# Values of the gated recurrence computed feature by feature and transposed on TensorE, with the output fetches, the query fetch and the copies moved in their queues

## The chip, the cores and the metric

The kernel is one program on one core of a Trainium2 chip. The metric is the time of one execution on the device, in microseconds (us), as the median of several runs. The engines are named as the profile names them: PE is TensorE (PEld its weight loads), DVE is VectorE, ACT is ScalarE, POOL is GpSimd, and SP is the queue engine that issues most DMAs. [...]

## The reference

Two transformer-like blocks run one after the other on 512 tokens of width 1024. The change is in the second block, whose sequence has 16 meta tokens in front (528 tokens, `T2`). After a norm the tokens `z` are projected and fed into two mixers:

```
z = rmsnorm(h, mix_norm_g)
p = z @ w_in                                  # u | q | f | i | og | ga | gb, 1024 columns each
y_a = s5_mixer(p[u], ...)                     # state space model
y_b = hgrn2_mixer(p[q], p[f], p[i], p[og], lb, norm_g)
merged = sigmoid(p[ga]) * (y_a @ w_ssm_proj) + sigmoid(p[gb]) * (y_b @ w_hgrn_proj)

# hgrn2_mixer, per head of 128 features, chunks of 16 tokens
f = lb + (1 - lb) * sigmoid(f_logit);  cum = cumsum(log f) within a chunk
q_in = q * exp(cum);  k_in = (1 - f) * exp(-cum);  v = i_in
scores = where(causal, q_in @ k_in.T, 0);  o = scores @ v + q_in @ state
state = decay * state + k_out.T @ v
```

The part `i` (`i_in`, the values `v`) is needed with tokens on the partitions (`Vt`); `q` and `f` are needed with features on the partitions.

## The kernel before, in words

**Products in parts.** Each f32 weight tile of 128 x 1024 (a unit, 512 KB) is fetched by SP into one of two `stage` buffers, copied by ACT into `whi` (`split_hi`, L912), and DVE makes the rest `wlo = stage - whi` (`split_lo`, L2153); there are four pairs `whi`/`wlo`. A job of PE is three products (`whi*zhi`, `whi*zlo`, `wlo*zhi`) for each of 8 k tiles, into two PSUM banks (one for each half of the tokens), picked by the job's parity. `marks` counts finished jobs; `emptied[parity]` says that the job's PSUM has been read out. `ahead(name, j)`, called by ACT and by DVE before they serve job `j`, splits the unit that takes the buffers of the job before (four units further on). SP loads a unit when the one two before it has been split. All engines run their own program strictly in order, so the order in which the calls stand is the order of the work.

**Order around the change.** Jobs `u`, `q`, `f` (8 each), then the values `i0`, `i1`, then 8 `ga` jobs with the state space outputs between them, then `i2`, `i3`, then 8 heads with two gate jobs each (`og`, `gb`), then `glu`. `i0` to `i3` are each 256 features: five jobs (one for each of five token tiles of 128, the last overlapping), in which the token tile is the stationary operand and 256 weight columns stream (L1998, 24 matmuls a job). ACT copies each job's 128 x 256 from PSUM straight into `Vt` (`value_job`, L1266).

**State space side.** DVE runs a scan of 64 steps (L2752, L2757, L2759) up to the middle of `i1`, and between its steps `skip(b)` finishes the kernel tile of block `b` (`k_done`). The Toeplitz tile `TT` of a block is made by 8 shifting DMAs: 4 from SP (`shifted`, L842), 4 from ACT (`k_shift`, L1283), both after `k_done`. `outputs(b)` on PE (L1975, L1982) needs them; ACT copies its result to `Y5` (L1315), SP stores it (`y_store`), and when all 8 are stored SP fetches them back turned, as 64 small DMAs (`y_rows`, L854), which ACT's gelu needs later.

**Gates.** POOL waits for the last `outputs`, issues the fetch of `f` into `KH` and of `q` into `QH` (4 DMAs each, L3109), zeroes `sT` and `kout` (L3112, L3113) and signals `rmask_done`, for which DVE waits before anything of `i2` and PE before the heads. ACT makes the logs of 8 heads (`gate_log`, L1325) in the first four jobs of `i2`; DVE then a scan for each head (L2813, L2815); ACT the two exponentials (`gate_exps`, L1332, L1334) one head in each job of `i3`, where head `h` waits for `dec_done` of head `h-2`; DVE `into_gates` (L2800 to L2806), `decays`, and in the heads `own_scores` and the other masks (`sT_done`). PE's head `h`: `head_scores` (L2028), a gate job, `head_keys` (four transposes, L2038), `head_second` (L2048), `head_third` (L2058), a gate job, `head_values` of the head before (L2090, L2096; not in head 0), `head_deltas` (L2073). ACT copies the transposed keys (`ko`, L1373) and spills the gate jobs (L1258).

Of the kernel before, what the change touches and what calls it, by code (L numbers as in the profile page):

```python
# [13 lines left out]
P = 128  # L14
# [19 lines left out]
HEADS = 8  # L34
# [170 lines left out]
SPILLED = ["q", "f", "ga", "og", "gb"]  # L205
# [3 lines left out]
def emit(nc, A, out):  # L209
# [4 lines left out]
    with ctx:  # L214
# [121 lines left out]
        kout4 = at("kout4", [P, T1], 4 * CONST["mla"])  # L336
        rmask = at("rmask", [P, T2], 4 * CONST["mla"])
# [108 lines left out]
        lb_in, lb_sig, lb_done = sem("lb_in"), sem("lb_sig"), sem("lb_done")  # L446
# [300 lines left out]
        def _(sp):  # L747
# [62 lines left out]
            def weights(name, j):  # L810

                c0 = {"u": 0, "q": 1024, "f": 2048, "og": 4096, "ga": 5120, "gb": 6144}
                if name[0] == "i":
                    c = 3072 + 256 * int(name[1])
                    return [(lambda s: s[:].rearrange("p (k c) -> p k c", k=4), w_in2[:, 4 * j:4 * j + 4, c:c + 256])]
# [87 lines left out]
        def _(act):  # L903
# [314 lines left out]
            def ssm_angles():  # L1218
                act.wait_ge(s5_vec, 2)
                act.activation(v5[:, 3, :], v5[:, 3, :], ACT.Exp).then_inc(s5_exp, 1)  # L1220
                act.wait_ge(s5_vec, 3)
                act.activation(v5[:, 7:9, :], v5[:, 7:9, :], ACT.Sin).then_inc(s5_sin, 1)
                act.wait_ge(lb_in, 1)
                act.activation(gsc[:, 2, :], gsc[:, 2, :], ACT.Sigmoid).then_inc(lb_sig, 1)
# [37 lines left out]
            def value_job(c, j):  # L1262

                n = J["i%d" % c] + j
                act.wait_ge(marks, plan.full[n])
                act.activation(Vt[:, j, c * 256:(c + 1) * 256], ps[:, 2 * (n % 2), 0:256], ACT.Copy)\  # L1266
                   .then_inc(emptied[n % 2], 1)
# [37 lines left out]
            for c in range(2):  # L1305
                for j in range(TB2):
                    ahead("i%d" % c, j)
                    if (c, j) == (0, 0):
                        k_evac(1)
                    elif (c, j) == (0, 3):  # L1310
                        k_shift(1)
                    value_job(c, j)
# [23 lines left out]
            act.wait_ge(lb_done, 1)  # L1336
            for j in range(TB2):
                ahead("i2", j)
                if j < 4:
                    gate_log(2 * j)  # L1340
                    gate_log(2 * j + 1)
                value_job(2, j)
            for j in range(TB2):
                ahead("i3", j)
                gate_exps(j)
                value_job(3, j)
            for h in range(TB2, HEADS):
                gate_exps(h)
# [19 lines left out]
            for h in range(HEADS):  # L1368
# [10 lines left out]
                if h == 1:  # L1379
                    act.wait_ge(yT_in, 16 * KD * KD)  # L1380
                if 1 <= h <= 4:
                    for k in (2 * h - 2, 2 * h - 1):
                        act.activation(y5[:, k, :], y5[:, k, :], ACT.Gelu_apprx_tanh).then_inc(gelu_done, 1)
# [70 lines left out]
        def _(pe):  # L1454
# [3 lines left out]
            def products(n, T, ks, w, x_hi, x_lo, fresh=None):  # L1458

                last = None  # L1460
                for b, t0, t1 in halves(T):
                    out = ps[:, 2 * (n % 2) + b, 0:t1 - t0]
# [8 lines left out]
            def gemm(name, j, x_hi, x_lo, T, ks=KD, i=None, fresh=None):  # L1471
# [7 lines left out]
                products(n, T, ks, lambda a, k: a[u % NHL][:, k * P:(k + 1) * P], x_hi, x_lo, fresh)\  # L1479
# [506 lines left out]
            def value_jobs(c):  # L1986

                name = "i%d" % c
                for j in range(TB2):
                    n = J[name] + j  # L1990
                    wait_emptied(pe, n)
                    out = ps[:, 2 * (n % 2), 0:256]
                    for k in range(KD):
                        uu, o = (U[name] + k // 4) % NHL, (k % 4) * 256
                        if j == 0 and k % 4 == 0:
                            pe.wait_ge(split_done, U[name] + k // 4 + 1)
                        for a, x in ((whi, zhi), (wlo, zhi), (whi, zlo)):
                            mm = pe.matmul(out, x[:, k, TS2[j]:TS2[j] + P], a[uu][:, o:o + 256],  # L1998
                                           start=(k == 0 and a is whi and x is zhi), stop=(k == KD - 1 and x is zlo))
                    mm.then_inc(marks, 1)  # L2000
# [6 lines left out]
            value_jobs(0)  # L2007
            value_jobs(1)
            for b in range(NB5):
                outputs(b)  # L2010
                gemm("ga", b, zx(zhi), zx(zlo), T3)
                if b + 2 < NB5:
                    kernels(b + 2)
            value_jobs(2)
            value_jobs(3)

# [45 lines left out]
            def head_deltas(h):  # L2062
# [4 lines left out]
                else:  # L2067
                    wait_job_out(pe, J["i3"] + TB2 - 2)
                    wait_job_out(pe, J["i3"] + TB2 - 1)
# [36 lines left out]
            for h in range(HEADS):  # L2106
                head_scores(h)
                gate_job(2 * h)
# [38 lines left out]
        def _(dve):  # L2147
# [467 lines left out]
            def ssm_params(step):  # L2615
# [3 lines left out]
                if step == 0:  # L2619
# [7 lines left out]
                                      ALU.subtract).then_inc(lb_in, 1)  # L2627
# [30 lines left out]
                elif step == 4:  # L2658
                    product_re(BB[:, 0, :, :], *bb)
                    dve.wait_ge(lb_sig, 1)  # L2660
                    link(dve.tensor_scalar(gsc[:, 3, :], gsc[:, 2, :], -1.0, 1.0, ALU.mult, ALU.add))
                    dve.tensor_scalar(gsc[:, 0, :], gsc[:, 3, :], -1.0, None, ALU.mult).then_inc(lb_done, 1)
# [121 lines left out]
            for c in range(2):  # L2784
                for j in range(TB2):
                    ahead("i%d" % c, j)
                    scan(52 + 2 * (TB2 * c + j), 54 + 2 * (TB2 * c + j))
                    if (c, j) == (0, 2):
                        skip(1)
# [18 lines left out]
            dve.wait_ge(rmask_done, 1)  # L2808
            for j in range(TB2):
                ahead("i2", j)  # L2810
            for h in range(HEADS):
# [5 lines left out]
            for j in range(TB2):  # L2817
                ahead("i3", j)
# [24 lines left out]
            for h in range(HEADS):  # L2843
                into_gates(h)
                if h == 0:
                    decays(0, 1)
# [137 lines left out]
        def _(pool):  # L2984
# [120 lines left out]
            for name, tiles, done in (("f", KH, hgate_in), ("q", QH, qgate_in)):  # L3105
                for k in range(4):
# [93 lines left out]
```

## Time and profile before

| what | value |
|---|---|
| median of 3 runs | 1754.97 us (1750.53 to 1756.06) |
| the profiled execution's own time | 1754.68 us |
| its span | 1752.9 us |
| PE busy | 1696.5 us, 97% of the span |
| DVE, ACT, POOL busy | 1092.1, 745.3, 297.7 us (62%, 43%, 17%) |
| share of PE in the chain that ended last | 83% |

The profile page gives shares over the whole span. The views of the trace place things: the timeline lists the instructions of an engine in order of time, and a value in brackets behind one is how long the engine was idle before it and what released it. All times in the trace count from the start of the span.

### The profile page before, as it was taken

Reading aid. Unit: us, or ns where it says so; the run is one execution under the profiler, and the core shown is the slowest. Engines: PE = TensorE matmul, PEld = TensorE weight load, DVE = VectorE, ACT = ScalarE, POOL = GpSimd, SP = SyncE. Lnnn points to the kernel's source line nnn. Section 1 sums busy time; section 2 is a strip of 40 time slices with the busy share of each in tenths; the row PEclk is TensorE's granted clock in tenths of the full one; section 3 lists DMA queues with packets and bytes.
Section 4 is the critical chain, followed back from the end, with each engine's and each line's share of the span. In section 5 each row is a group of like instructions: output and inputs, shape, how many; then the busy total and the mean of one; then the engine's idle time right before and its main releaser. Section 6 shows DMA issues by size and latency. Waiting matters only on the chain.

```text
span 1752.9 us, 32409 instructions
## 1 busy us (share of the span) xinstructions
PE 1696.5 (97%) x12781; PEld 1506.5 (86%) x12781; DVE 1092.1 (62%) x1748; ACT 745.3 (43%) x1111; POOL 297.7 (17%) x286
## 2 busy tenths in 40 slices
PE   5999999999999999999999999999999999999998
PEld 4776756788888888799999999999999999989986
DVE  6756476677664577865868664343753766654633
ACT  4367575365332342632323545447233643322323
POOL 2112197310000001532005221210102000000002
PEclk8999999999999999999999999999999999999999
DMA  9363542433333332264435752332543233332332
GB/s 313 101 151 97 157 120 73 144 88 102 99 96 98 94 96 75 70 180 126 129 105 145 232 145 83 96 122 75 170 116 97 71 87 95 92 100 85 96 94 75
DMA packets 321167, 201.18 MB, mean 115 GB/s; under 512 B 51279, under 2 KB 303814, under 8 KB 320918
## 3 DMA queue, kind: packets, MB, share of 16 engines
q1 hardware_dynamic: 300976, 160.79, 32.3%
q0 software_dynamic: 7952, 24.83, 4.7%
q10 hardware_dynamic: 12118, 13.88, 2.3%
q8 instruction: 85, 1.39, 0.3%
q14 instruction: 36, 0.29, 0.1%
HBM read 177.75 MB, written 17.24 MB: 111 GB/s over the span
## 4 chain that ended last, share of the span: by engine, by line
PE 83%; DVE 6%; ACT 4%; SPq 2%; issue 2%; DMA 1%; POOL 1%; ACTq 0%; DVEq 0%; POOLq 0%
PE ps L1467 69%; SPq L854 2%; DVE wlo L2153 1%; PE ps L1608 1%; PE ps L1768 1%; PE ps L1794 1%; PE ps L1778 1%; PE ps L1667 1%; PE ps L1998 1%; PE ps L1682 1%; PE ps L1584 1%; ACT whi L912 1%; DMA xrow<-in_x_dram 1%; PE ps L1924 0%; PE ps L1536 0%
## 5 line engine op out<-in xcount | busy, mean ns | idle before, releaser
L1467 PE MATMUL ps<-zhi,whi 128*128 128x258 f32 (+2 forms) x2072 | 639.3, 309 | 2.8 <-DVE wlo L2153 1.4
L1467 PE MATMUL ps<-zlo,whi 128*128 128x258 f32 (+2 forms) x2072 | 634.0, 306 | 0.0
L1467 PE MATMUL ps<-zhi,wlo 128*128 128x258 f32 (+2 forms) x2072 | 632.7, 305 | 0.0
L1467 PEld LDWEIGHTS ps<-zhi,whi 128*128 128x128 f32 x2072 | 391.2, 189 | 27.7 <-DVE wlo L2153 2.9
L2153 DVE TENSOR_TENSOR wlo<-stage,whi 128x1024 fp32r<-128x1024 f32 x256 | 322.7, 1262 | 139.0 <-ACT whi L912 127.0
L1467 PEld LDWEIGHTS ps<-zlo,whi 128*128 128x128 f32 x2072 | 390.5, 188 | 19.5 <-issue 1.0
L1467 PEld LDWEIGHTS ps<-zhi,wlo 128*128 128x128 f32 x2072 | 391.1, 189 | 18.2
L912 ACT ACTIVATE whi<-stage 128x1024 fp32r<-128x1024 f32 x256 | 269.4, 1055 | 314.8 <-PE ps L1467 260.3
L1467 PE MATMUL ps<-ghi,whi 128*128 128x512 f32 x340 | 134.7, 396 | 0.0
L1467 PE MATMUL ps<-glo,whi 128*128 128x512 f32 x340 | 134.2, 395 | 0.0
L1467 PE MATMUL ps<-ghi,wlo 128*128 128x512 f32 x340 | 134.0, 394 | 0.0
L1201 ACT ACTIVATE ub<-ps 128x512 f32<-128x512 f32 (+1 forms) x88 | 52.6, 597 | 162.7 <-PE ps L1467 161.4
L3036 POOL TENSOR_TENSOR zu<-zu,sq 128x528 f32<-128x528 f32 (+1 forms) x18 | 31.6, 1758 | 425.5 <-ACT sq L920 424.6
L2566 DVE TENSOR_SCALAR cv<-ub,par 128x512 f32<-128x512 f32 (+1 forms) x88 | 49.0, 556 | 70.2 <-ACT ub L1201 70.2
L1211 ACT ACTIVATE ghi<-cv 128x512 f32 (+1 forms) x44 | 27.9, 634 | 124.4 <-DVE cv L2581 124.4
L1467 PEld LDWEIGHTS ps<-ghi,wlo 128*128 128x128 f32 x340 | 64.0, 188 | 15.0
L1467 PEld LDWEIGHTS ps<-ghi,whi 128*128 128x128 f32 x340 | 63.9, 188 | 14.7
L1467 PEld LDWEIGHTS ps<-glo,whi 128*128 128x128 f32 x340 | 63.9, 188 | 14.6
L2575 DVE SCALAR_TENSOR_TENSOR cv<-ub,par,cv 128x512 f32<-128x512 f32 (+1 forms) x88 | 66.3, 754 | 13.1 <-DVE cv L2569 6.7
L3029 POOL TENSOR_SCALAR pb<-pb,small 128x128 f32<-128x128 f32 (+3 forms) x64 | 72.8, 1156 | 9.5 <-DVE small L2456 9.2
L2482 DVE TENSOR_TENSOR xT<-ps,xT 128x512 f32 (+2 forms) x30 | 20.8, 692 | 85.1 <-PE ps L1467 85.1
L1258 ACT ACTIVATE spill<-ps 128x516 f32<-128x516 f32 (+1 forms) x40 | 24.1, 604 | 103.4 <-PE ps L1467 103.3
(426 smaller groups left out, 2836.2 us busy)
## 6 DMA issues: line engine op xcount, KB each, us to landing
stage<-in_w_up_dram SPq DMA_DIRECT2D x88, 512.0 KB, 3.8
stage<-in_w_in_dram SPq DMA_DIRECT2D x74, 512.0 KB, 4.0
stage<-in_w_down_dram SPq DMA_DIRECT2D x32, 512.0 KB, 4.0
ring<-in_w_ada_dram POOLq DMA_DIRECT2D x24, 512.0 KB, 4.4
adab<-in_w_ada_dram SPq DMA_DIRECT2D x16, 512.0 KB, 8.3
stage<-in_w_down_dram SPq DMA_DIRECT2D x16, 384.0 KB, 3.4
stage<-in_w_o_dram SPq DMA_DIRECT2D x8, 512.0 KB, 3.9
ring<-in_w_ada_dram SPq DMA_DIRECT2D x8, 512.0 KB, 3.8
```

What stands on the lines that cost most here:

```text
L854: sp.dma_start(y5[SH * g:SH * g + SH, k, :].rearrange("p (j c) -> p j c", j=LC), y_view[g])\
L912: act.activation(whi[u % NHL][:], stage[slot][:], ACT.Copy).then_inc(hi_done, 1)
L1201: act.activation(wide(ub[:, j % 2, 2:2 + T], T), acc(job, T), ACT.Copy).then_inc(emptied[job % 2], 1)
L1211: act.activation(ghi[c % 2][:, bass.ds(i * 2 + q, 1), 0:T].rearrange("p a t -> p (a t)"), cv[:, q, 1, 0:T], ACT.Copy).then_inc(ghi_done, 1)
L1258: act.activation(wide(spill[m % 2][:, T2 - T:T2], T), acc(n, T), fn).then_inc(emptied[n % 2], 1)
L1467: last = pe.matmul(out, w(a, k), x(k, t0, t1), start=(k == 0 and a is whi and x is x_hi), stop=(k == ks - 1 and a is wlo))
L2153: dve.tensor_tensor(wlo[u % NHL][:], stage[plan.w_load[u] % NST][:], whi[u % NHL][:].bitcast(F32), ALU.subtract).then_inc(split_done, 1)
L2482: ins = dve.tensor_tensor(x, acc(job, T), x, ALU.add)
L2566: link(dve.tensor_scalar(o, ub[:, g, 2:2 + T], tap(2), par[:, bass.ds(i * 2 + (ROW[f["cb"]] + ft), 1)], ALU.mult, ALU.add))
L2575: dve.scalar_tensor_tensor(out=o, in0=ub[:, g, 0:T], scalar=tap(0), in1=o, op0=ALU.mult, op1=ALU.add).then_inc(conv_done, 1)
L3029: pool.tensor_scalar(pb[:, t % 4, r, 0:w], pb[:, t % 4, r, 0:w], total(t, r, 32), None, ALU.mult)\
L3036: pool.tensor_tensor(square(n, 0), square(n, 0), square(n, 1 + j % 2), ALU.add).then_inc(acc_done, 1)
```

## The change

The values are now two groups of four ordinary jobs, `ia` and `ib` (128 features each, features on the partitions). ACT copies a job's result from PSUM to one of four column buffers `vcol` (`value_out`). PE transposes it with five f32 transposes back into the PSUM of the same job (`value_turn`), in the middle of the next job, between its two halves (`between`); the turns of values 3 and 7 stand behind `outputs(0)` and `head_scores(0)`. ACT then copies the turned tiles to `Vt` with two copies (`value_rows`) and frees the PSUM, and this copy stands ahead of the split of the next unit. The logs and exponentials are dealt out over the four jobs of `ib` (four heads, four heads, two, two). POOL fetches `q` only after job `ib` 0. `y_rows` are fetched in four pairs, each behind one unit of `og`. SP issues `shifted(1)` ahead of the loads of `ga` 0 and 1. The gelu of the state space outputs begins one head later.

```diff
-    p.shared("i0", 2, TB2)
-    p.shared("i1", 2, TB2)
+    p.gemm("ia", 4)
     p.gemm("ga", 8)
-    p.shared("i2", 2, TB2)
-    p.shared("i3", 2, TB2)
+    p.gemm("ib", 4)
...
+GATE_LOGS = [(0, 1, 2, 3), (4, 5, 6, 7), (), ()]
+GATE_EXPS = [(), (), (0, 1), (2, 3)]
...
+        vcol = [at("vcol0", [P, T2], ZUO + 2 * row), at("vcol1", [P, T2], RSO)] + spill
...
+        def value_no(m):
+            return (J["ia"] + m) if m < 4 else (J["ib"] + m - 4)
+        def value_cols(m):
+            return vcol[m % 2 + 2 * (m // 4)]
...
# SP
-            loads("i0", 0, 2)
+            loads("ia", 0, 2)
             shifted(0)
-            loads("i1", 0, 2)
+            loads("ia", 2, 4)
+            shifted(1)
             loads("ga", 0, 2)
-            shifted(1)
             loads("ga", 2, 4)
...
-                name, j = (("ga", b + 4) if b < 4 else ("i2", b - 4) if b < 6 else ("i3", b - 6))
+                name, j = ("ga", b + 4) if b < 4 else ("ib", b - 4)
                 loads(name, j, j + 1)
             y_store(NB5 - 1)
             loads("og", 0, 2)
             sp.wait_ge(ys_out, 16 * KD)
-            for k in range(6):
-                y_rows(k)
-            loads("og", 2, 3)
-            y_rows(6)
-            loads("og", 3, 4)
-            y_rows(7)
-            loads("og", 4, 8)
+            for k in range(4):
+                loads("og", k + 2, k + 3)
+                y_rows(2 * k)
+                y_rows(2 * k + 1)
+            loads("og", 6, 8)
...
# ACT
+            def value_out(m):
+                n = value_no(m)
+                act.wait_ge(marks, plan.full[n])
+                if m % 4 >= 2:
+                    act.wait_ge(vt_mm, m - 1)
+                if m in (4, 5):
+                    wait_spilled(act, "ga", m + 2)
+                act.activation(wide(value_cols(m)[:, :], T2), acc(n, T2), ACT.Copy).then_inc(vcol_done, 1)
+            def value_rows(m):
+                s = 2 * (value_no(m) % 2)
+                act.wait_ge(vt_mm, m + 1)
+                act.activation(Vt[:, 0:4, m * P:(m + 1) * P], ps[:, s, :].rearrange("p (b d) -> p b d", b=4), ACT.Copy)
+                act.activation(Vt[:, 4, m * P:(m + 1) * P], ps[:, s + 1, 0:P], ACT.Copy)\
+                   .then_inc(emptied[value_no(m) % 2], 1)
...
+            for m in range(4):
+                if m:
+                    value_rows(m - 1)
+                ahead("ia", m)
+                if m == 0:
+                    k_evac(1)
+                elif m == 1:
+                    k_shift(1)
+                value_out(m)
             for b in range(NB5):
...
                 ahead("ga", b)
+                if b == 0:
+                    value_rows(3)
...
+            for m in range(4, 8):
+                if m > 4:
+                    value_rows(m - 1)
+                ahead("ib", m - 4)
+                for h in GATE_LOGS[m - 4]:
+                    gate_log(h)
+                for h in GATE_EXPS[m - 4]:
+                    gate_exps(h)
+                value_out(m)
+            gate_exps(4)
+            value_rows(7)
+            for h in range(5, HEADS):
                 gate_exps(h)
...
# PE
+            def value_turn(m):
+                pe.wait_ge(vcol_done, m + 1)
+                n = value_no(m)
+                for b, t0 in enumerate(TS2):
+                    mm = pe.transpose(ps[:, 2 * (n % 2) + b // 4, (b % 4) * P:(b % 4) * P + P], value_cols(m)[:, t0:t0 + P],
+                                      const("ident"))
+                mm.then_inc(vt_mm, 1)
+            def value_job(m):
+                gemm("ia" if m < 4 else "ib", m % 4, zx(zhi), zx(zlo), T2,
+                     between=(lambda: value_turn(m - 1)) if m % 4 else None)
...
             for h in range(HEADS):
                 head_scores(h)
+                if h == 0:
+                    value_turn(7)
                 gate_job(2 * h)
...
# DVE
+            for m in range(4):
+                ahead("ia", m)
+                if m == 0:
+                    scan(52, 55)
+                    skip(1)
+                    scan(55, 57)
+                else:
+                    scan(52 + 5 * m, 57 + 5 * m)
...
+            dve.wait_ge(rmask_done, 1)
+            for m in range(4):
+                ahead("ib", m)
+                if m < 2:
+                    for h in range(4 * m, 4 * m + 4):
+                        gate_scan(h)
+                elif m == 2:
+                    into_gates(0)
+                    decays(0, 1)
+                    into_gates(1)
+            for h in range(2, HEADS):
                 into_gates(h)
-                if h == 0:
-                    decays(0, 1)
                 if h == 6:
                     own_scores(0)
...
# POOL
             for name, tiles, done in (("f", KH, hgate_in), ("q", QH, qgate_in)):
+                if name == "q":
+                    pool.wait_ge(marks, plan.full[J["ib"]])
                 for k in range(4):
...
+            pool.wait_ge(vt_mm, 4)
             pool.memset(kout[:, 0:T1], 0.0).then_inc(rmask_done, 1)
```

## Rows read from the trace of the kernel before

**Rows 1.** The profile page, first part: busy time of each engine.

```profile
PE 1696.5 (97%) x12781; PEld 1506.5 (86%) x12781; DVE 1092.1 (62%) x1748; ACT 745.3 (43%) x1111; POOL 297.7 (17%) x286
```

**Rows 2.** Timeline of PE: start, duration, line, count, idle before and its releaser.

```profile
889.39 0.39 PE L1998 MATMUL ps<-whi,zhi 128*128 128x256 f32 x1
...
904.94 0.39 PE L1998 MATMUL ps<-whi,zhi 128*128 128x256 f32 x1 [1.08 <-ACT Vt L1266]
...
919.34 1.16 PE L1975 MATMUL ps<-U,TT 128*64 128x66 f32 x32
...
937.96 1.16 PE L1975 MATMUL ps<-U,TT 128*64 128x66 f32 x32 [1.15 <-DMA TT<-K]
...
1017.32 1.19 PE L2028 MATMUL ps<-QH,KH 128*128 128x128 f32 x10
```

**Rows 3.** Waits of PE from 800 to 1200 us: total, times, longest.

```profile
PE ps L2073 <- ACT ko L1373: 1.4, 1, 1.4
...
PE ps L2028 <- DVE sT L2886: 0.6, 1, 0.6
```

**Rows 4.** The chain that ended last, from 800 to 1200 us.

```profile
1034.96 1.26 PE ps L2028 x10
```

**Rows 5.** Timeline of PE in head 1, gate jobs left out.

```profile
1041.89 0.60 PE L2038 MATMUL ps<-cst,kout 128*128 128x128 f32 x4
1042.42 0.69 PE L2048 MATMUL ps<-QH,KH 128*64 128x64 f32 x16
```

**Rows 6.** Timeline of ACT in jobs f and i0.

```profile
858.86 0.61 ACT L1258 ACTIVATE spill<-ps 128x528 f32<-128x528 f32 x1 [3.73 <-PE ps L1467]
...
864.71 0.61 ACT L1258 ACTIVATE spill<-ps 128x528 f32<-128x528 f32 x1 [3.72 <-PE ps L1467]
...
901.40 3.06 ACTq L1283 DMA_DIRECT2D TT<-K  x4
```

**Rows 7.** Timeline of SP: start, time until the last issue ended.

```profile
901.34 2.51 SPq L842 DMA_DIRECT2D TT<-K  x4
...
993.69 27.99 SPq L854 DMA_DIRECT2D y<-y_scratch  x48
```

**Rows 8.** The tile stage from 860 to 990 us: issue to landing of a unit.

```profile
DMA to landing us min/median/max: 3.5/4.9/14.9
```

**Rows 9.** Timeline of DVE in i0.

```profile
894.12 0.31 DVE L2752 TENSOR_TENSOR sc<-AA,S 128x128 f32<-128x128 f32 x1
...
899.84 0.27 DVE L2734 TENSOR_TENSOR dtmp<-cst,Dg 16x128 f32<-16x128 f32 x1
```

**Rows 10.** Timeline of POOL at the start of i2.

```profile
987.42 2.89 POOL L3109 DMA_DIRECT2D QH<-q_scratch  x4
...
991.45 0.55 POOL L3113 MEMSET kout<- 128x512 f32 x1
```

**Rows 11.** Timeline of DVE in i2, i3 and head 0.

```profile
992.02 1.23 DVE L2153 TENSOR_TENSOR wlo<-stage,whi 128x1024 fp32r<-128x1024 f32 x1 [5.97 <-POOL kout L3113]
...
1009.79 0.70 DVE L2800 TENSOR_TENSOR QH<-QH,ex 128x528 f32<-128x528 f32 x1
...
1027.40 1.22 DVE L2153 TENSOR_TENSOR wlo<-stage,whi 128x1024 fp32r<-128x1024 f32 x1
```

**Rows 12.** Timeline of ACT in i2 and i3.

```profile
989.13 0.60 ACT L1258 ACTIVATE spill<-ps 128x516 f32<-128x516 f32 x1 [4.34 <-PE ps L1467]
...
1015.06 0.65 ACT L1334 ACTIVATE LF<-LF 128x528 f32<-128x528 f32 x1
```

**Rows 13.** Windows of 2 us: length, busy and count of PE, PEld, DVE, ACT, POOL; granted clock; DMA.

```profile
730.00:732.00 2.00, 0.96 (x4) 0.61 (x5) 2.00 (x6) 1.54 (x5) 0.00 (x0) 1.00 0.01 4
...
1360.00:1362.00 2.00, 1.13 (x8) 0.83 (x7) 2.00 (x6) 1.98 (x4) 0.00 (x0) 0.98 0.00 0
1362.00:1364.00 2.00, 2.00 (x12) 2.00 (x11) 1.62 (x5) 1.97 (x6) 0.00 (x0) 0.50 0.00 0
1364.00:1366.00 2.00, 2.00 (x13) 2.00 (x13) 1.24 (x5) 1.99 (x4) 0.00 (x0) 0.67 0.00 0
```

More of the change, by code:

```diff
@@ L445, in emit @@
                                                          sem("ylo_done"), sem("ya_done"))
-        lb_in, lb_sig, lb_done = sem("lb_in"), sem("lb_sig"), sem("lb_done")
+        lb_step = sem("lb_step")
+        vcol_done, vt_mm = sem("vcol_done"), sem("vt_mm")
         lf_done, cum_done, ep_done, em_done, kin_done, dec_done = (
@@ L810, in weights @@
             def weights(name, j):
[L812 to L815, printed above, removed]
+                c0 = {"u": 0, "q": 1024, "f": 2048, "ia": 3072, "ib": 3584, "og": 4096, "ga": 5120, "gb": 6144}
                 if name in c0:
@@ L1222, in ssm_angles @@
                 act.activation(v5[:, 7:9, :], v5[:, 7:9, :], ACT.Sin).then_inc(s5_sin, 1)
-                act.wait_ge(lb_in, 1)
-                act.activation(gsc[:, 2, :], gsc[:, 2, :], ACT.Sigmoid).then_inc(lb_sig, 1)
+                act.wait_ge(lb_step, 1)
+                act.activation(gsc[:, 2, :], gsc[:, 2, :], ACT.Sigmoid).then_inc(lb_step, 1)
             def into_columns(b):
@@ L1304, in _ @@
                     k_shift(0)
[L1305 to L1312, printed above, removed]
+            for m in range(4):
[7 more added lines that the diff above has]
+                value_out(m)
             for b in range(NB5):
@@ L1334, in gate_exps @@
                 act.activation(LF[:, h, :], LF[:, h, :], ACT.Exp, scale=-1.0).then_inc(em_done, 1)
[L1336 to L1347, printed above, removed]
+            act.wait_ge(lb_step, 3)
+            for m in range(4, 8):
[10 more added lines that the diff above has]
+            for h in range(5, HEADS):
                 gate_exps(h)
@@ L1378, in _ @@
                     heads_out(h - 1)
-                if h == 1:
+                if h == 2:
                     act.wait_ge(yT_in, 16 * KD * KD)
-                if 1 <= h <= 4:
-                    for k in (2 * h - 2, 2 * h - 1):
+                if 2 <= h <= 5:
+                    for k in (2 * h - 4, 2 * h - 3):
                         act.activation(y5[:, k, :], y5[:, k, :], ACT.Gelu_apprx_tanh).then_inc(gelu_done, 1)
@@ L1456, in job, with products @@
                 pass
-            def products(n, T, ks, w, x_hi, x_lo, fresh=None):
+            def products(n, T, ks, w, x_hi, x_lo, fresh=None, between=None):
                 last = None
                 for b, t0, t1 in halves(T):
+                    if b and between:
+                        between()
                     out = ps[:, 2 * (n % 2) + b, 0:t1 - t0]
@@ L1469, in products, with gemm @@
                 return last
-            def gemm(name, j, x_hi, x_lo, T, ks=KD, i=None, fresh=None):
+            def gemm(name, j, x_hi, x_lo, T, ks=KD, i=None, fresh=None, between=None):
                 n, u = J[name] + j, U[name] + j
@@ L1478, in gemm @@
                     wait_emptied(pe, n, i)
-                products(n, T, ks, lambda a, k: a[u % NHL][:, k * P:(k + 1) * P], x_hi, x_lo, fresh)\
+                products(n, T, ks, lambda a, k: a[u % NHL][:, k * P:(k + 1) * P], x_hi, x_lo, fresh, between)\
                     .then_inc(marks, 1)
@@ L1984, in outputs @@
                 mm.then_inc(y_mm, 1)
[L1986 to L2000, printed above, removed]
+            def value_turn(m):
[8 more added lines that the diff above has]
+                     between=(lambda: value_turn(m - 1)) if m % 4 else None)
             for j in range(8):
@@ L2006, in _ @@
             kernels(1)
-            value_jobs(0)
-            value_jobs(1)
+            for m in range(4):
+                value_job(m)
             for b in range(NB5):
                 outputs(b)
+                if b == 0:
+                    value_turn(3)
                 gemm("ga", b, zx(zhi), zx(zlo), T3)
@@ L2013, in _ @@
                     kernels(b + 2)
-            value_jobs(2)
-            value_jobs(3)
+            for m in range(4, 8):
+                value_job(m)
             def head_scores(h):
@@ L2067, in head_deltas @@
                 else:
-                    wait_job_out(pe, J["i3"] + TB2 - 2)
-                    wait_job_out(pe, J["i3"] + TB2 - 1)
+                    wait_job_out(pe, value_no(6))
+                    wait_job_out(pe, value_no(7))
                 for b in range(4):
@@ L2626, in ssm_params @@
                     dve.tensor_tensor(gsc[:, 2, :], par[:, ROW["lb"]:ROW["lb"] + 8], par[:, ROW["lb"] + 8:ROW["lb"] + 16],
-                                      ALU.subtract).then_inc(lb_in, 1)
+                                      ALU.subtract).then_inc(lb_step, 1)
                 elif step == 1:
@@ L2783, in _ @@
                     skip(0)
[L2784 to L2789, printed above, removed]
+            for m in range(4):
[6 more added lines that the diff above has]
+                    scan(52 + 5 * m, 57 + 5 * m)
             for b in range(NB5):
@@ L2806, in into_gates, with gate_scan @@
                 dve.tensor_tensor(KH[:, h, :], KH[:, h, :], LF[:, h, :], ALU.mult).then_inc(kin_done, 1)
[L2808 to L2811, printed above, removed]
+            def gate_scan(h):
                 dve.wait_ge(lf_done, h + 1)
@@ L2816, in _ @@
                    .then_inc(cum_done, 1)
-            for j in range(TB2):
-                ahead("i3", j)
             def decays(h0, h1):
@@ L2841, in own_scores @@
                                     ps[:, 4, :].rearrange("p (b t) -> p b t", b=4)).then_inc(sT_done, 1)
-            for h in range(HEADS):
+            dve.wait_ge(rmask_done, 1)
+            for m in range(4):
+                ahead("ib", m)
[7 more added lines that the diff above has]
+            for h in range(2, HEADS):
                 into_gates(h)
-                if h == 0:
-                    decays(0, 1)
                 if h == 6:
```

8 lines of the change are left out of this document (2 added, 6 removed).

## Prediction, made before the changed kernel was run

> **What bounds the kernel now.** I read the page first: PE is busy 97% of the span [rows 1], so the end moves only with PE's own work and its gaps. The view of waits, cut to the stretch of the change, then shows how small its gaps are: about 5 us in 400, among them 2.0 us in head 0 [rows 3]. The timeline of PE gives the two stretches that the change rebuilds. The values `i0`, `i1` take from 889.39 to `outputs(0)` at 919.34, 29.95 us with a wait of 1.08 us in it; `i2`, `i3` take from the end of `ga` 7 at 989.1 to the first `head_scores` at 1017.3, 28.2 us without a gap [rows 2, 12]. Last I read the queues of ACT, SP, DVE and POOL in the same stretches, because each engine works in its written order, and a PE with short gaps can be held by any of them.
>
> **PE's work.** An ordinary job of 48 products takes 5.86 us (from spill to spill, 858.86 to 864.71) [rows 6]. Four transposes of the same form as the new ones take 0.53 us from their start to that of the next group [rows 5], so five take 0.66 us; if each took its full 0.27 us one behind the other it would be 1.35 us, which is the upper end. The group of four values with its three inner turns is 4 x 5.86 + 3 x 0.66 = 25.4 us, against 28.9 us (29.95 less the wait) and 28.2 us before. With the two outer turns of 0.66 us the work of PE falls by 3.5 + 2.8 - 1.3 = 5.0 us. That is the gain if nothing is late.
>
> The Trainium skill (TensorE: Matmul & The Clock Gate, Part 4: PE-mode transpose) gives about 275 ns for one 128 x 128 transpose inside a kernel. Taken as a spacing it would make 40 of them 11.0 us instead of 5.3 us; the rows agree with it as the length of one, but their starts lie closer.
>
> **The group ia: ACT is held by a load.** `shifted(1)` now stands ahead of the load of `ga` 0 in SP's queue, and it waits for `k_done`. Before, DVE ended six steps of the scan between 894.12 and 899.84 (0.95 us each), and the shifts went out at 901.34 [rows 9, 7]. Now three steps stand ahead, so they go out at 898.5 and SP is free 2.5 us later, at 901.0. Only then is the load of `ga` 0 issued; a unit lands 3.5 to 4.9 us after its issue [rows 8], I take 4.5 us: 905.5. ACT's queue for `ia` 1 is: `value_rows(0)` (done about 899.7), the split of `ga` 0, `k_shift(1)`, `value_out(1)`. The split waits for the landing and ends at 906.6; the four issues of `k_shift` take 3.06 us [rows 6], to 909.8; the copy of 0.6 us ends at 910.4. PE wants turn 1 at 889.39 + 2 x 5.86 + 0.66 + 2.93 = 904.7. It stands still for 5.8 us (4.8 to 6.2 over the range of landings), in the middle of job `ia` 2. What was behind cover before: the split of `ga` 0 came only at `i1`, long after its landing. DVE is queued behind the same split; it ends its last scan step at about 916, before `outputs(0)`. The group then takes 25.4 + 5.8 = 31.2 us instead of 29.95: 1.25 us lost.
>
> In the `ga` stage the 1.15 us that PE waits at 937.96 for shifted tiles [rows 2] shrink, since DVE has one split (1.2 us) less ahead of `skip(2)`; but turn 3 (0.66 us) and the output of `kernels` after it push the same chain. From `outputs(0)` to `outputs(2)` I count 0.36 us won. The rest of that stage keeps its order.
>
> **The group ib: DVE is held by POOL.** Let T be the start of `ib` 0 (989.1 in the old trace, by the end of `ga` 7 [rows 12]). POOL's queue is `f` fetch, `q` fetch, memsets, `rmask_done`. From the first issue of `q` at 987.42 to the last memset's end at 992.0 are 4.6 us [rows 10]. The `q` fetch now waits for the end of `ib` 0, T + 5.9, so `rmask_done` comes at T + 10.5 instead of T + 2.9. DVE has its wait for it in front of everything of `ib`: the split, eight scans, two more splits, the gates. From there to the first `into_gates` were 17.8 us (992.02 to 1009.79) [rows 11], with the same eight scans and three splits as now: T + 28.3. From that to the end of ACT's exponentials of head 3 were 5.9 us (1009.79 to 1015.71) [rows 11, 12]: T + 34.2. In the old order nothing of PE hung on them. Now `value_out(7)` stands behind the exponentials of heads 2 and 3, turn 7 behind `value_out(7)`, and the first gate job behind turn 7. The copy ends at T + 34.8, the turn at T + 35.5. PE's own work would bring it there at T + 25.4 + 1.2 + 0.66 = T + 27.3. A smaller wait lies inside: `value_out(6)` stands behind a split, a table load and four exponentials, and turn 6 waits some 0.6 us for it; it is covered by the larger one.
>
> Before, the first gate job started at T + 29.4. It is 6.1 us late. Of this 2.0 us come back, the two waits of head 0 [rows 3]: they came from 48 `y_rows` issues in one piece (28 us, 0.58 us each [rows 7]) ahead of `og` 2 and 3, and 16 of them between units cost 9.3 us, less than two gate jobs. With 5.9 us for head 0 less those waits, `head_scores(1)` stands at T + 50.0 instead of T + 45.9 (1034.96 [rows 4]): 4.1 us lost. DVE's gates and decays ended at 1027.40, T + 38.3 [rows 11]; 7.6 us later and with one more split between them they end at T + 47, and the split of `og` 3 and two masks (2.2 us) make it ready for `head_scores(1)` at T + 49, so it is not far from being the bound itself. Later heads have no wait that I find: each `og` unit lands before its split is wanted.
>
> **The clock.** Both stalls end in a long gap of PE: 5.8 us in `ia`, and in `ib` 3.7 us idle, 1.2 us of `head_scores`, 3.7 us idle. In the old trace the granted clock was 0.50 and 0.67 (the 1.2 GHz level) in the two windows from 1362, after PE had been busy 1.13 of 2 us from 1360; that is 1.7 us of work lost. But from 730 to 732 PE was busy 0.96 of 2 us and the clock stayed at 1.00 [rows 13]. I take one such loss for each stall, 2 x 1.7 = 3.4 us, with 0 and 3.4 us as ends.
>
> The Trainium skill (TensorE: Matmul & The Clock Gate, Why this matters for your kernels) warns that a long gap between bursts of matmuls puts the array back at half rate. By it both stalls cost the loss above, as in the sum; without it the sum would be 3.4 us smaller. The trace of before holds a case of each kind.
>
> **The rest at nothing.** The column copies and `value_rows` (0.6 and 0.8 us) are ACT's, which has gaps of over 3 us in each job; without them they would cost PE a wait at each turn. The gelu one head later has four heads of slack. The number of units and bytes is the same.
>
> **The sum.** 1.25 - 0.36 + 4.1 = 5.0 us, and 3.4 us for the clock: 8.4 us. The profiled execution took 1754.7 us (span 1752.9 and 1.8 around it), close to the median of 1755.0. Predicted: 1763.1 us.
>
> **Rivals.**
> - *No loss of clock (0.20).* Stalls as above, but the array keeps 2.4 GHz, for which the windows at 730 speak: 1754.7 + 5.0 = 1759.7.
> - *One of the two stalls is covered (0.16).* If the load of `ga` 0 lands or the shifts go out far earlier, 5.8 + 1.7 us fall away: 1755.6. If instead DVE's chain does not reach PE, `ib` costs 27.3 instead of 35.5 us and the clock holds: 8.2 + 1.7 less, 1753.2.
> - *Faster (0.13).* Neither chain binds: PE gains its 5.0 us of work, the 1.1 us wait of `i0`, about 1 us of the tile wait and the 2.0 us of head 0: 9.1 us, 1745.6. For it speaks that PE is the bound nearly everywhere [rows 1]. The mechanism is PE's work alone; it decides if `value_out(7)` ends by T + 26.6, that is if ACT's exponentials of head 3 come 8 us sooner than I count, and if `ga` 0 has landed by 900. The chain of DVE would have to shrink from 17.8 to 10 us for that.
> - *Worse (0.07).* Full-length transposes (40 x 0.14 = 5.6 us more, some of it inside the stalls) or DVE and `og` units late in head 1, over 1767.
>
> The forecast holds 0.44, its own range 1760.5 to 1766. The range that leaves out 2 in 10 goes from the covered cases to just above the forecast's end: 1750 to 1767. A difference of 0.3% (5.3 us) is about what a measurement of this kernel can tell from no change. Slower by more than that, over 1760.2: the forecast, the worse case and 0.08 of the case without a loss of clock, together 0.59. Within it: the covered cases and the rest of that one, 0.28. Faster, below 1749.7: 0.13.
>
> **What the profile would show.** Right: a wait of PE of 5 to 6 us at a transpose in `ia`, behind ACT's column copy, with ACT's split before it waiting for the DMA of `stage`; DVE waiting for POOL's memset of `kout` some 13 us (6.0 before); a wait of PE of about 3.5 us at `head_scores(0)` and one as long at the turn behind it; a granted clock of 0.5 in the windows behind each; no waits at L2073 in head 0. Wrong: transposes over 0.2 us apart; `ga` 0 landed before 901; `rmask_done` within 4 us of T; or waits of PE in the heads after the first.

## The result, and the profile after

The changed kernel takes 1762.17 us (median of five, 1761.0 to 1762.67) against 1754.97 us (also of five): a ratio of 1.004 with a 95% interval of 1.0029 to 1.0051. It is slower by 0.4%, 0.9 us below the forecast of 1763.1. Its profiled execution has a span of 1760.8 us, 7.9 us more than before.

First the page, its busy times; PE's total is the same as before to 0.3 us [rows 1] although it has less to do, because part of it ran slower.

```profile
PE 1696.8 (96%) x12725; PEld 1506.8 (86%) x12725; DVE 1092.5 (62%) x1748; ACT 748.6 (43%) x1115; POOL 299.1 (17%) x286
```

The waits of PE between 750 and 1250 us (in total, times, longest). The two waits of head 0 [rows 3] and the tile wait [rows 2] are gone. In their place stand four new ones: one at turn 1 and two at turns 6 and 7 (all L2013), and one at `head_scores(0)` (L2050). The last line of the view was there before too.

```profile
PE ps L2013 <- ACT vcol L1275: 4.2, 1, 4.2
PE ps L2013 <- ACT spill L1275: 3.7, 2, 2.3
PE ps L2050 <- issue: 3.4, 1, 3.4
PE ps L2112 <- ACT QH L1384: 0.9, 1, 0.9
```

The timeline of ACT in `ia` 1. The split (L917) has waited 5.5 us for its DMA; the shift issues and the column copy of value 1 (L1275) stand behind it. (ACTq and SPq are the DMA issues of ACT and of SP.)

```profile
899.17 0.27 ACT L1282 ACTIVATE Vt<-ps 128x128 f32<-128x128 f32 x1
904.97 1.06 ACT L917 ACTIVATE whi<-stage 128x1024 fp32r<-128x1024 f32 x1 [5.53 <-DMA stage<-in_w_in_dram]
905.03 2.99 ACTq L1299 DMA_DIRECT2D TT<-K  x4
908.08 0.61 ACT L1275 ACTIVATE vcol<-ps 128x528 f32<-128x528 f32 x1 [2.05 <-issue]
```

The timeline of SP shows why: the shifts now go out at 898.1 (901.34 before [rows 7]), and the unit of `ga` 0 only behind them.

```profile
898.09 2.52 SPq L849 DMA_DIRECT2D TT<-K  x4
900.66 12.92 SPq L713 DMA_DIRECT2D stage<-in_w_in_dram  x4
```

The timeline of PE, the turns of values 1 and 2, then the outputs, then the second place (turn 6, `head_scores(0)`, turn 7) and head 0 up to `head_scores(1)`.

```profile
908.74 1.33 PE L2013 MATMUL ps<-cst,vcol 128*128 128x128 f32 x5 [4.23 <-ACT vcol L1275]
...
917.94 0.71 PE L2013 MATMUL ps<-cst,vcol 128*128 128x128 f32 x5
...
921.49 1.16 PE L1997 MATMUL ps<-U,TT 128*64 128x66 f32 x32
...
1013.54 0.77 PE L2013 MATMUL ps<-cst,spill 128*128 128x128 f32 x5 [1.35 <-ACT spill L1275]
...
1020.63 2.28 PE L2050 MATMUL ps<-QH,KH 128*128 128x128 f32 x10 [3.41 <-issue]
...
1025.22 1.33 PE L2013 MATMUL ps<-cst,spill 128*128 128x128 f32 x5 [2.31 <-ACT spill L1275]
1034.11 0.60 PE L2060 MATMUL ps<-cst,kout 128*128 128x128 f32 x4
1034.70 0.69 PE L2070 MATMUL ps<-QH,KH 128*64 128x64 f32 x16
...
1042.80 1.29 PE L2050 MATMUL ps<-QH,KH 128*128 128x128 f32 x10
```

The timeline of DVE in `ib` and head 0 answers to [rows 11]: 13.75 us of idleness until POOL's last memset, then 17.5 us of scans and splits to the first gate (17.8 before), and `own_scores(0)` (L2863) that ends at 1034.65, just as PE wants it at L2070.

```profile
1001.31 1.23 DVE L2177 TENSOR_TENSOR wlo<-stage,whi 128x1024 fp32r<-128x1024 f32 x1 [13.75 <-POOL kout L3147]
...
1018.77 0.70 DVE L2826 TENSOR_TENSOR QH<-QH,ex 128x528 f32<-128x528 f32 x1
...
1033.93 0.72 DVE L2863 COPY_PREDICATED sT<-cst,ps 128x512 f32<-128x512 int32 x1
```

Windows of 2 us behind each gap (columns as in [rows 13]). The granted clock is the third value from the end: 1.00 is the 2.4 GHz level, 0.50 the 1.2 GHz level, and a value between them is a window that holds both.

```profile
905.00:907.00 2.00, 0.00 (x0) 0.00 (x0) 0.94 (x1) 1.03 (x1) 0.00 (x0) 1.00 0.48 118
907.00:909.00 2.00, 0.26 (x1) 0.26 (x2) 1.83 (x7) 0.61 (x1) 0.00 (x0) 0.74 0.27 67
909.00:911.00 2.00, 2.00 (x11) 2.00 (x11) 1.79 (x7) 0.90 (x3) 0.00 (x0) 0.50 0.81 228
911.00:913.00 2.00, 2.00 (x11) 2.00 (x11) 1.90 (x5) 0.81 (x1) 0.00 (x0) 0.50 0.00 0
913.00:915.00 2.00, 2.00 (x12) 2.00 (x12) 1.83 (x7) 0.00 (x0) 0.00 (x0) 0.55 0.24 58
```

```profile
1020.00:1022.00 2.00, 1.37 (x6) 1.40 (x7) 1.93 (x9) 1.29 (x2) 0.74 (x1) 0.65 0.89 259
1022.00:1024.00 2.00, 0.91 (x6) 0.80 (x4) 1.97 (x4) 0.64 (x1) 2.00 (x3) 0.50 0.67 125
...
1028.00:1030.00 2.00, 2.00 (x11) 2.00 (x10) 1.93 (x6) 1.81 (x5) 0.00 (x0) 0.50 0.46 109
1030.00:1032.00 2.00, 2.00 (x15) 2.00 (x15) 1.93 (x5) 1.62 (x3) 0.00 (x0) 0.79 1.05 266
```

**Where the time went**, stretch by stretch, from starts in the two timelines. T is the start of ACT's spill of `ga` 7, 989.13 before and 990.64 after; `ia` 0 starts at 889.39 and 889.03.

| stretch | before | after | difference | predicted |
|---|---|---|---|---|
| `ia` 0 to `outputs(0)` | 29.95 | 32.46 | +2.5 | +1.25, +1.7 clock |
| `outputs(0)` to `outputs(2)` (939.40) | 18.62 | 17.91 | -0.7 | -0.4 |
| `outputs(2)` to T | 51.17 | 51.24 | +0.1 | 0 |
| T to `head_scores(1)` | 45.83 | 52.16 | +6.3 | +4.1, +1.7 clock |
| sum | | | +8.2 | +8.4 |

With 0.4 us less before `ia` that is the 7.9 us of the spans.

### The profile page after: what moved, and what is told of

Same layout as the page of the kernel before. It is cut to its first block, busy times and chain, and to the rows that moved or that the text cites. A ratio compares the mean times of both kernels' runs of the same rounds, so it can differ in the third digit from the quotient of the medians.

```text
span 1760.8 us, 32312 instructions
## 1 busy us (share of the span) xinstructions
PE 1696.8 (96%) x12725; PEld 1506.8 (86%) x12725; DVE 1092.5 (62%) x1748; ACT 748.6 (43%) x1115; POOL 299.1 (17%) x286
## 4 chain that ended last, share of the span: by engine, by line
PE 84%; DVE 7%; ACT 4%; issue 1%; DMA 1%; POOL 1%; SPq 0%; ACTq 0%; DVEq 0%
PE ps L1489 70%; DVE wlo L2177 1%; PE ps L1630 1%; PE ps L1790 1%; PE ps L1816 1%; PE ps L1800 1%; PE ps L1689 1%; PE ps L1704 1%; PE ps L1606 1%; ACT whi L917 1%; DVE LF L2837 1%; DMA xrow<-in_x_dram 1%; PE ps L2004 1%; DMA stage<-in_w_in_dram 0%; PE ps L2095 0%
## 5 line engine op out<-in xcount | busy, mean ns | idle before, releaser
L1489 PE MATMUL ps<-zhi,whi 128*128 128x258 f32 (+2 forms) x2200 | 678.8, 309 | 2.4 <-DVE wlo L2177 1.0
L1489 PE MATMUL ps<-zlo,whi 128*128 128x258 f32 (+2 forms) x2200 | 672.2, 306 | 0.0
L1489 PE MATMUL ps<-zhi,wlo 128*128 128x258 f32 (+2 forms) x2200 | 671.1, 305 | 0.0
L1489 PEld LDWEIGHTS ps<-zhi,whi 128*128 128x128 f32 x2200 | 417.6, 190 | 27.4 <-DVE wlo L2177 2.7
L1489 PEld LDWEIGHTS ps<-zlo,whi 128*128 128x128 f32 x2200 | 416.9, 190 | 19.6 <-issue 1.0
L1489 PEld LDWEIGHTS ps<-zhi,wlo 128*128 128x128 f32 x2200 | 417.3, 190 | 18.2
L917 ACT ACTIVATE whi<-stage 128x1024 fp32r<-128x1024 f32 x256 | 269.7, 1054 | 310.8 <-PE ps L1489 260.2
```

What stands on the lines that cost most here:

```text
L917: act.activation(whi[u % NHL][:], stage[slot][:], ACT.Copy).then_inc(hi_done, 1)
L1489: last = pe.matmul(out, w(a, k), x(k, t0, t1), start=(k == 0 and a is whi and x is x_hi), stop=(k == ks - 1 and a is wlo))
```

## Experiments

The first theory is the one of the prediction: two stalls, each made by a queue order that the new way of making values does not need. Its main rival is that the new values cost PE or ACT as much as they save.

**shift_behind.**

```diff
             loads("ia", 2, 4)
-            shifted(1)
             loads("ga", 0, 2)
+            shifted(1)
             loads("ga", 2, 4)
```

> The changed kernel with one edit taken back: SP issues shifted(1) behind the loads of ga 0 and 1 again. My theory (ACT's split of ga 0 is held by a load that stands behind the shifts): the wait of PE at turn 1 (4.2 us) falls under 0.5 us and with it the 5.6 us at the 1.2 GHz level behind it (2.8 us of work lost), so 7.0 us less than the changed kernel: about 1755.2. Rival (ACT's own queue is too full in ia, the load only hides it): the wait at turn 1 stays over 2 us and the time over 1759.

Measured: 1755.68 us, 1.0006 of the kernel before (0.9997 to 1.0014), 6.5 us less than the changed kernel (7.0 expected). PE's wait at turn 1 is gone altogether, and the clock is 1.00 in every window from 899 to 917. `ia` 0 to `outputs(0)` takes 25.3 us (888.45 to 913.73), against 28.9 in the old way without its wait. ACT's timeline, where the split no longer waits:

```profile
898.59 0.27 ACT L1282 ACTIVATE Vt<-ps 128x128 f32<-128x128 f32 x1
898.74 1.06 ACT L917 ACTIVATE whi<-stage 128x1024 fp32r<-128x1024 f32 x1
899.17 1.94 ACTq L1299 DMA_DIRECT2D TT<-K  x3
901.15 0.61 ACT L1275 ACTIVATE vcol<-ps 128x528 f32<-128x528 f32 x1 [1.35 <-PE ps L1489]
```

ACT's own queue is not too full: it waits for PE. The load behind the shifts is the cause of the first stall.

**zeros_first.**

```diff
             for name, tiles, done in (("f", KH, hgate_in), ("q", QH, qgate_in)):
                 if name == "q":
+                    for k in range(2):
+                        pool.memset(sT[k][:, :, :], 0.0)
+                    pool.wait_ge(vt_mm, 4)
+                    pool.memset(kout[:, 0:T1], 0.0).then_inc(rmask_done, 1)
                     pool.wait_ge(marks, plan.full[J["ib"]])
...
-            for k in range(2):
-                pool.memset(sT[k][:, :, :], 0.0)
-            pool.wait_ge(vt_mm, 4)
-            pool.memset(kout[:, 0:T1], 0.0).then_inc(rmask_done, 1)
```

> The changed kernel with POOL's memsets and rmask_done put ahead of the fetch of q, which keeps its wait for job ib 0. My theory (DVE is held by rmask_done alone): DVE begins at T + 3 instead of T + 10.7, into_gates(0) comes at T + 20.7, the waits of PE at head_scores(0) and turn 7 (3.4 and 2.3 us) shrink to under 2 us together, and with the clock behind them 8 to 9 us are won: about 1753.5. Rival (the late fetch of q itself holds DVE): into_gates(0) waits for q until beyond T + 25 and under 4 us are won, over 1758.

Measured: 1755.65 us, 1.0002 (0.9994 to 1.0011), 6.5 us less than the changed kernel, where 8 to 9 were expected. DVE begins at T + 2.2, and the first `into_gates` starts at T + 20.7 (1009.42, T being 988.77). The waits at `head_scores(0)` and turn 7 fall to 0 and 0.8 us. The timeline of DVE, its first `into_gates`:

```profile
1009.42 0.70 DVE L2826 TENSOR_TENSOR QH<-QH,ex 128x528 f32<-128x528 f32 x1
```

What I had not expected is the wait of PE at L2070:

```profile
PE ps L2013 <- ACT vcol L1275: 3.9, 1, 3.9
PE ps L2070 <- DVE sT L2863: 2.3, 1, 2.3
PE ps L2013 <- ACT spill L1275: 1.1, 2, 0.8
```

The L2013 line with 3.9 us is the stall in `ia`, untouched here. At L2070, `head_second` of head 0 waits for `own_scores(0)`, which DVE does only behind `into_gates(6)`.

**queries_early.** The wait of POOL ahead of the `q` fetch taken out (two lines).

> The changed kernel without the wait that POOL has ahead of the fetch of q. By my theory the same time as with the memsets first, within 1.5 us (about 1753.5), since both let DVE begin at T + 3. Rival (fetching q later wins something of its own, less traffic beside the other fetches): over 2 us slower than with the memsets first.

Measured: 1756.05 us, 1.0009 (0.9999 to 1.0018), within 0.4 us of zeros_first, with the same waits (2.5 us at L2070). So the late fetch as such neither costs nor wins anything that shows; what it pushed back was `rmask_done`.

**both_mended.** The edits of shift_behind and zeros_first together.

> Both edits: shifted(1) behind the loads of ga 0 and 1, and the memsets ahead of the fetch of q. The two stalls are 100 us apart, so by my theory their gains add up: 7.0 + 8.5 us less than the changed kernel, about 1746.5, faster than the kernel before by 8 us. That is PE's smaller work (5.0 us by the prediction) and the waits that the kernel before had. Rival (the new way of making the values costs PE as much as the old one): not below 1752.

Measured: 1748.07 us, 0.9959 (0.9946 to 0.9971). The gains add up: 6.5 and 6.5 alone, 14.1 together (15.5 expected). The time is under the 1752 of the rival, and `ia` 0 to `outputs(0)` takes 25.3 us here too, so the new way of making values costs PE less than the old one. Left are 2.3 us at L2070 and 1.1 us at turns 6 and 7, and one more loss, behind the wait at L2070, which ends at 1020.04:

```profile
1020.00:1022.00 2.00, 1.96 (x33) 1.85 (x33) 1.86 (x6) 1.60 (x2) 0.00 (x0) 0.52 0.44 72
1022.00:1024.00 2.00, 2.00 (x12) 2.00 (x12) 2.00 (x6) 1.06 (x1) 1.52 (x2) 0.62 0.70 195
```

The clock fell behind this wait too, and behind the 2.5 us of queries_early, but in the profile of zeros_first it stayed at 1.00 behind the same 2.3 us. With the fall `head_scores(1)` comes at T + 46.2 and T + 46.4, without it at T + 44.7: about 1.5 us.

**filler_in_stall.** To price the clock by itself, PE gets unread work where it stood still.

```diff
             def value_turn(m):
+                if m == 1:
+                    for i in range(34):
+                        pe.matmul(ps[:, 4, 0:HT2], zhi[:, i % KD, 0:P],
+                                  zhi[:, i % KD, 0:HT2], start=True, stop=True)
                 pe.wait_ge(vcol_done, m + 1)
```

> The changed kernel with 34 products of 128 x 264, whose result nobody reads, put in front of PE's wait at turn 1 (4.2 us idle in the changed kernel, 34 x 0.122 = 4.1 us of work), so that PE is busy where it stood still; the added work is output to an unused PSUM bank. If the 5.6 us at the 1.2 GHz level behind that wait come from PE's idleness, the granted clock stays at 1.00 there and 2.8 us are won: about 1759.4. Rival (the lower clock there has another cause): clock and time as in the changed kernel, 1762.

Measured: 1760.26 us, 1.0025 (1.0015 to 1.0036), 1.9 us less than the changed kernel, where 2.8 were expected. In the windows:

```profile
907.00:909.00 2.00, 2.00 (x18) 1.94 (x16) 1.86 (x6) 0.42 (x1) 0.00 (x0) 1.00 0.19 38
909.00:911.00 2.00, 1.91 (x17) 1.76 (x16) 1.79 (x7) 1.15 (x4) 0.00 (x0) 1.00 0.91 254
911.00:913.00 2.00, 2.00 (x18) 2.00 (x18) 1.86 (x6) 0.80 (x2) 0.00 (x0) 1.00 0.01 3
```

The clock stays at its upper level. From turn 1 to turn 2 are 6.5 us (909.24 to 915.71) against 9.2 in the changed kernel (908.74 to 917.94): the fall of the clock costs 2.7 us of time here, and it is PE's idleness that brings it. The filler did not push the turn: it starts 19.7 us after `ia` 0 in both (889.51 and 889.03). Of the 2.7 us, 0.5 are lost again before `outputs(2)` (18.4 us from `outputs(0)` against 17.9); the cause of that is not shown.

**copy_ahead_of_exps.** `value_out(7)` ahead of the exponentials of heads 2 and 3 in ACT's queue.

```diff
+                if m == 7:
+                    value_out(m)
                 for h in GATE_EXPS[m - 4]:
                     gate_exps(h)
-                value_out(m)
+                if m < 7:
+                    value_out(m)
```

> The changed kernel with one swap in ACT's queue: value_out(7) ahead of the exponentials of heads 2 and 3. Rival A (ACT's order is what binds): turn 7 no longer waits (2.3 us), PE starts the first gate job at T + 32 instead of T + 35, and 3 to 5 us are won, 1757 to 1759. My theory (DVE, late by rmask_done, binds right behind it): own_scores(0) still ends at T + 43, so the wait moves to head_second of head 0 (L2070) with 4 to 5 us, and at most 1.5 us are won, about 1761.

Measured: 1764.47 us, 1.0044 (1.0029 to 1.0059): nothing won, and by the spans 2.1 us lost, where up to 1.5 won were expected. The wait moved as my theory said:

```profile
PE ps L2073 <- DVE sT L2866: 4.5, 1, 4.5
PE ps L2016 <- ACT vcol L1275: 4.0, 1, 4.0
PE ps L2053 <- issue: 3.6, 1, 3.6
```

L2073 is `head_second` here. PE came earlier to it and stood there 4.5 us, until T + 44.1, when it started this work in the changed kernel too, and behind that second idleness the clock fell again, now in `og` 1:

```profile
1030.00:1032.00 2.00, 0.00 (x0) 0.00 (x0) 1.93 (x5) 1.58 (x4) 0.00 (x0) 1.00 0.95 226
1032.00:1034.00 2.00, 0.00 (x0) 0.00 (x0) 1.90 (x6) 1.98 (x4) 0.00 (x0) 0.89 0.42 74
1034.00:1036.00 2.00, 1.80 (x32) 1.79 (x32) 1.90 (x6) 1.76 (x2) 0.00 (x0) 0.50 0.43 69
1036.00:1038.00 2.00, 2.00 (x13) 1.90 (x10) 1.97 (x7) 1.06 (x1) 1.36 (x2) 0.50 0.53 170
```

`head_scores(1)` stands at T + 54.9 (1045.02 less 990.11), not at T + 52.2: from `head_second` on it takes 10.8 us instead of 8.1.

**filler_in_three_gaps.** The filler at turn 1, 26 such products ahead of `head_scores(0)` and 18 ahead of turn 7.

> The changed kernel with unread products of 128 x 264 in all three gaps of PE: 34 ahead of turn 1 (as in the run before), 26 ahead of head_scores(0) (3.4 us idle, 3.2 us of work) and 18 ahead of turn 7 (2.3 us idle, 2.2 us of work). By my theory the stalls stay as they are and only the 10 us at the 1.2 GHz level behind the second gap go: the first gate job takes 5.9 us again instead of 7.9, another 2.0 us less than with the filler at turn 1 alone (1760.3), about 1758.3. Rival (the clock there does not matter, since DVE is as late): 1760.

Measured: 1760.62 us, 1.0029 (1.0019 to 1.004). The rival is right and I was wrong. The clock was 1.00 through both gaps and the first gate job, but PE then waited 2.5 us at `head_second` (L2077 here) for `own_scores(0)`, and the clock fell behind that wait:

```profile
PE ps L2077 <- DVE sT L2872: 2.5, 1, 2.5
```

```profile
1034.00:1036.00 2.00, 2.00 (x11) 2.00 (x11) 1.97 (x7) 1.06 (x1) 0.93 (x2) 0.50 0.64 185
```

The 1.2 GHz level behind the second stall cost nothing of its own in the changed kernel: DVE was as late. `head_second` starts at T + 44.1 with it (changed kernel, shift_behind, filler_in_stall) and without it. PE's wait at `head_scores(0)` is here put down to DVE's `KH`, in the 1.3 us that are left of it behind the filler (L2057); the profile of the changed kernel names no releaser for it.

**copy_and_mask_ahead.** copy_ahead_of_exps, and in DVE's queue `own_scores(0)` behind `into_gates(3)` instead of `into_gates(6)`.

> The run with value_out(7) ahead of the exponentials (1764.5, PE waited 4.5 us at head_second for own_scores) and DVE's own_scores(0) behind into_gates(3) instead of into_gates(6). If DVE's late chain is what binds, that wait falls to 1 to 2 us and the next one shows at head_scores(1) or behind it; together 3 to 4 us are won against that run and 1 to 2 us against the changed kernel: about 1760.5. If instead the order in DVE was the only obstacle, no new wait appears and the time is under 1758.5.

Measured: 1759.23 us, 1.0024 (1.0013 to 1.0035), 5.2 us less than without the second edit and 2.9 less than the changed kernel, more than the 3 to 4 and 1 to 2 expected. No wait at `head_second` is left, and one of 1.7 us stands at `head_scores(1)` (L2053), for the last masks of head 0, at T + 49.3 (1038.61 less 989.29):

```profile
PE ps L2053 <- DVE sT L2920: 1.7, 1, 1.7
```

It is what DVE's chain allows after a start at T + 10.7: the prediction had T + 49 for it.

**rows_between_old.** The kernel before with `y_rows` in four pairs between the `og` units, and the gelu one head later, as in the change.

> The kernel before with one part of the change alone: y_rows in four pairs between the og units, and the gelu one head later. My theory: the two waits of PE in head 0 (1.4 us at L2073, 0.6 us at L2028) fall away, 2.0 us won, about 1753.3. Rival (the load comes sooner but DVE or another load takes its place): the waits stay in another form and the time is that of the kernel before.

Measured: 1754.93 us, 0.9991 (0.9981 to 1.0002): no difference. The two waits of head 0 are gone, and another one of the same size has come, at `head_scores(2)` (L2026), through ACT:

```profile
PE ps L2026 <- ACT QH L1362: 2.2, 1, 2.2
```

```profile
1048.84 1.06 ACT L910 ACTIVATE whi<-stage 128x1024 fp32r<-128x1024 f32 x1 [7.01 <-DMA stage<-in_w_in_dram]
```

ACT waits 7.0 us for `og` 6, whose load now stands behind 16 of the small fetches and goes out at 1044.81, and PE waits 2.2 us, until 1051.61, for ACT's copies behind that split. Up to `head_scores(1)` the edit does win its 2 us (T + 43.7 instead of T + 45.8); the order moves the stall from one unit to another in the old kernel. In the changed kernel and in all its variants no such wait is seen. The load of `og` 6 goes out 12.3 us ahead of `head_scores(2)` in the changed kernel (1048.17 and 1060.49) and 10.4 us ahead in four_edits; here it is 4.6 us ahead of the time at which PE wants it. Which part of the change gives that room was not tested by itself.

**four_edits.** both_mended, `value_out` ahead of the exponentials in `ib` 2 and 3, and `own_scores(0)` behind `into_gates(4)`.

> Both mended (shifted(1) behind the loads, memsets ahead of the fetch of q) and two more edits against the waits that were left there: value_out ahead of the exponentials in jobs ib 2 and 3 (turns 6 and 7 waited 1.1 us), and DVE's own_scores(0) behind into_gates(4) instead of into_gates(6) (head_second waited 2.3 us for it). If those waits fall away without new ones, 3.4 us less than both mended: about 1744.6. If DVE is bound further on, a wait appears at head_scores(1) and the time stays over 1746.5.

Measured: 1746.14 us, 0.994 (0.9927 to 0.9953): 8.6 us less than the kernel before and 16 less than the changed one. It wins 1.9 us on both_mended where 3.4 were expected, and part of that can be the clock, which is 1.00 in every window from 1012 to 1050 here; `head_second` still waits 1.0 us and `head_scores(1)` 0.5 us, for DVE. `head_scores(1)` is at T + 42.6 (45.8 before).

## Why the prediction was right, point by point

- **PE's own work.** Right in size: `ia` takes 25.3 us where nothing waits (25.4 predicted). A turn costs 0.6 us (917.94 to 921.49, less half a job of 2.93), not 0.66; the five transposes start about 0.1 us apart, though each record is near 0.27 us long. That a transpose would take its full length in the stream was wrong.
- **The load behind the shifts.** Shown by shift_behind. I had PE's gap as 5.8 us; it was 4.2. The unit landed 0.5 us sooner than I took, and I put the shift issues behind the end of the split, beside which they ran: the first issue is at 905.03, the split from 904.97 to 906.03.
- **DVE held by POOL's memset.** Shown by zeros_first and queries_early. DVE began at T + 10.7 (T + 10.5 predicted), its first gate came at T + 28.1 (T + 28.3), ACT's copy ended at T + 34.5 (T + 34.8).
- **The clock.** In `ia` it cost 2.7 us where I had taken 1.7 from one case of before, and filler_in_stall shows idleness as the cause. That one case was a poor model: ahead of 1362 PE had stood still for 1.3 us and, at 1361.20, for 0.9 us, not for a time like that of the stalls.

```profile
1359.66 0.67 PE L1561 MATMUL ps<-sq,cst 128*128 128x258 f32 x2 [1.26 <-ACT sq L929]
```

The rule of the Trainium skill (TensorE: Matmul & The Clock Gate, Why this matters for your kernels), that a long gap between matmuls halves the clock, holds at both gaps (4.2 and 3.4 us). That is not all: the clock also fell behind shorter ones, the 2.3 us of both_mended and the 2.5 us of queries_early, and not behind the 2.3 us of zeros_first. In `ib` the fall came as said, with 10 us at the lower level from 1020.7 to 1030.8, but its price was hidden.

- **The step that was incomplete** is "DVE is ready for it at about T + 49, so it is not far from being the bound itself". I looked at DVE's last mask, wanted at `head_scores(1)`, and not at its first, `own_scores(0)`, wanted 8 us earlier at `head_second`. It ended at T + 44.0, when PE at full clock was there at T + 41.6 (filler_in_three_gaps, 44.1 less its wait of 2.5). So of the 6.3 us lost behind T about 2.5 are that mask or, in the run as it was, the clock, for which the prediction had 1.7. The term for the clock in `ib` is thus no loss of its own: without the fall the mask costs as much.
- **Two waits of head 0 come back.** They are gone in the changed kernel, and rows_between_old shows that the order of the fetches does it up to `head_scores(1)` (T + 43.7 instead of 45.8). Alone that edit still wins nothing, since 2.2 us are lost at `head_scores(2)`; in the changed kernel they are not.
- **What was luck.** That the sum came within 0.9 us owes something to errors that cancel: in `ia` the gap was put 1.6 us too long and the clock 1.0 us too cheap, and in `ib` the wait for `own_scores(0)`, which stood in no term, costs about what the clock was given.
- **Rivals.** "Faster" (1745.6) was the right price for the case in which nothing binds: four_edits, which comes close to it, has 1746.1. "No loss of clock" fell with the windows. "One stall covered" gave 1755.6 and 1753.2; the two runs gave 1755.7 and 1755.65. The second price is 2.4 us too low: with DVE's start mended the mask of head 0 still holds PE, for 2.3 us.

## What to carry to other kernels

An engine that works in written order turns every wait into a wait of all that stands behind it: before an instruction is moved ahead of a load, or a fetch ahead of a signal, list what the queue holds behind it, and who needs that. Here 5 us of saved work were lost to two such lines, and putting both back in order made it a gain of 7. And price a chain to each of its consumers, not only to the last: a second-latest engine takes over at once when the latest is freed, so that a mending edit alone can do nothing (copy_ahead_of_exps), or harm.

## What the runs showed of the hardware

- DMA issues of ACT's queue began while an activation of the same engine was still running (905.03 against 904.97 to 906.03), so issue time and compute time don't simply add. In shift_behind the first issue (898.24) began even before the split that stands ahead of it in the program (898.74), during the copy from 898.09. The next activation did wait for the last issue.
- A gap of 4.2 us in PE cost 2.7 us more behind it, through the granted clock. One of 2.3 us at `head_second` was followed by a fall in both_mended (0.52 and 0.62 in the next two windows) and by none in zeros_first; so variants of one kernel can differ by about 1.5 us by the clock alone. After the gaps around `head_scores(0)`, with little work between them, the 1.2 GHz level lasted for 10 us.
- Waiting later can be worse than waiting earlier. The same delay of DVE met PE in the changed kernel in gaps close together (3.4 and 2.3 us), with one stretch at the 1.2 GHz level whose cost was hidden. In copy_ahead_of_exps it met PE in gaps of 3.6 and 4.5 us with a gate job between them, and the clock fell twice, the second time with nothing to hide it (1762.9 against 1760.8 us of span).
